# Second layer's attention scores: one head's high and low parts in three products, masks first, turns behind the scores

## What is computed

```
q = concat([rmsnorm(q_nope), rope(rmsnorm(q_pe))])        # 64 + 32 = 96 per head
k = concat([rmsnorm(k_nope), rope(rmsnorm(k_pe))])        # k_pe is one for all heads
s = einsum('bqhd,bkhd->bhqk', qi, k) * scale              # 128 queries at a time
s = where(k_idx <= q_idx, s, -inf)
y = softmax(s) @ v
```

## Time and profile before

| | us |
|---|---|
| median of 3 runs | 2078.09 |
| lowest and highest | 2077.10, 2079.25 |
| the profiled execution, its own time | 2086.7 |
| its span, first to last instruction | 2084.9 |
| TensorE busy in the span | 2047.9 (98%) |
| GpSimd busy | 1515.2 (73%) |
| VectorE busy | 798.8 (38%) |
| ScalarE busy | 503.9 (24%) |

### The profile page before, as it was taken

The page is one execution under the profiler, slowest core; times in us unless marked ns, Lnnn a source line. Parts: engine busy times, 40 slices in busy tenths (PEclk is TensorE's granted clock), DMA queues, the critical chain, the costliest instruction groups (busy, mean ns, idle before and its releaser), DMA issues.

```text
span 2084.9 us, 25564 instructions
## 1 busy us (share of the span) xinstructions
PE 2047.9 (98%) x9848; PEld 1680.3 (81%) x9848; DVE 798.8 (38%) x1254; ACT 503.9 (24%) x981; POOL 1515.2 (73%) x820
## 2 busy tenths in 40 slices
PE   8999999999999999999999999899999999999997
PEld 7888888888888677888888887787788878888887
DVE  4342222211346664222211144865346334555202
ACT  6122111111354543211111133133201142222101
POOL 7787777877877526777878877443588888787775
PEclk9999999999999999999999999999999999999999
DMA  5232323333332102323333332111233322322232
GB/s 171 81 101 91 101 91 101 102 99 90 106 87 91 54 21 72 105 91 101 92 105 100 98 95 90 51 61 47 66 101 91 106 71 102 100 97 95 95 97 82
DMA packets 73884, 187.48 MB, mean 90 GB/s; under 512 B 12096, under 2 KB 27848, under 8 KB 73800
## 3 DMA queue, kind: packets, MB, share of 16 engines
q1 hardware_dynamic: 72632, 183.96, 27.7%
q10 hardware_dynamic: 1168, 2.35, 0.4%
HBM read 184.18 MB, written 2.10 MB: 89 GB/s over the span
## 4 chain that ended last, share of the span: by engine, by line
PE 94%; DVE 3%; ACT 1%; DMA 1%; POOL 1%; issue 1%; SPq 0%; DVEq 0%; ACTq 0%
PE stream_bank L1002 29%; PE stream_bank L1003 29%; PE stream_bank L1004 29%; PE stream_bank L1365 1%; PE work_bank L1695 0%; PE work_bank L1613 0%; DVE s_arena L3007 0%; DMA s_ring<-in_w_even 0%; POOL s_ring_low L829 0%; DVE s_arena L2980 0%; PE work_bank L1403 0%; DVE s_arena L2989 0%; PE work_bank L973 0%; PE work_bank L1714 0%; PE work_bank L1671 0%
## 5 line engine op out<-in xcount | busy, mean ns | idle before, releaser
L827 POOL TENSOR_TENSOR s_ring_high<-s_ring,s_zero 128x1024 fp32r<-128x1024 f32 (+1 forms) x359 | 652.4, 1817 | 487.1 <-DMA s_ring<-in_w_up 132.8
L829 POOL TENSOR_TENSOR s_ring_low<-s_ring,s_ring_high 128x1024 fp32r<-128x1024 f32 (+1 forms) x359 | 825.1, 2298 | 28.1
L1002 PE MATMUL stream_bank<-s_hn,s_ring_high 128*128 128x512 f32 x1682 | 660.8, 393 | 5.0 <-ACT s_arena L2208 2.1
L1004 PE MATMUL stream_bank<-s_hn,s_ring_low 128*128 128x512 f32 x1682 | 655.5, 390 | 0.0
L1003 PE MATMUL stream_bank<-s_hn,s_ring_high 128*128 128x512 f32 x1682 | 655.4, 390 | 0.0
L1002 PEld LDWEIGHTS stream_bank<-s_hn,s_ring_high 128*128 128x128 f32 x1682 | 315.7, 188 | 76.2 <-issue 4.0
L1004 PEld LDWEIGHTS stream_bank<-s_hn,s_ring_low 128*128 128x128 f32 x1682 | 315.7, 188 | 66.7
L1003 PEld LDWEIGHTS stream_bank<-s_hn,s_ring_high 128*128 128x128 f32 x1682 | 315.9, 188 | 65.0 <-issue 0.2
L1002 PE MATMUL stream_bank<-s_act,s_ring_high 128*128 128x512 f32 (+1 forms) x572 | 213.4, 373 | 0.4 <-POOL s_ring_low L829 0.4
L1003 PE MATMUL stream_bank<-s_act,s_ring_high 128*128 128x512 f32 (+1 forms) x572 | 213.2, 373 | 0.0
L1004 PE MATMUL stream_bank<-s_act,s_ring_low 128*128 128x512 f32 (+1 forms) x572 | 213.2, 373 | 0.0
(11 more groups left out here) (454 smaller groups left out, 2356.6 us busy)
## 6 DMA issues: line engine op xcount, KB each, us to landing
s_ring<-in_w_up SPq DMA_DIRECT2D x132, 512.0 KB, 3.5
s_ring<-in_w_down SPq DMA_DIRECT2D x24, 512.0 KB, 3.5
s_ring<-in_w_merge SPq DMA_DIRECT2D x24, 512.0 KB, 3.5
s_ring<-in_w_down SPq DMA_DIRECT2D x24, 448.0 KB, 3.3
s_ring<-in_w_ple SPq DMA_DIRECT2D x20, 512.0 KB, 3.5
s_ring<-in_w_even SPq DMA_DIRECT2D x15, 512.0 KB, 3.5
s_ring<-in_w_odd SPq DMA_DIRECT2D x13, 512.0 KB, 3.6
s_ring<-in_w_down SPq DMA_DIRECT2D x24, 256.0 KB, 2.8
```

The costliest lines, as they stand in the source:

```text
L827: nc.gpsimd.tensor_tensor(hi, ring[:, s, 0:n], zero[:].to_broadcast([P, n]), ALU.add).then_inc(w_high, 1)
L829: nc.gpsimd.tensor_tensor(ring_low[:, s, 0:n], ring[:, s, 0:n], hi.bitcast(F32), ALU.subtract).then_inc(split_ready[s], 1)
L1002: nc.tensor.matmul(o, w(0), x(0), start=start, stop=False)
L1004: return nc.tensor.matmul(o, w(1), x(0), start=False, stop=stop)
```

## The change

Queries and keys of one head at a time are kept in `qk`, four planes of 128 partitions and 512 tokens in the place of `qT` and `kT`: queries high (0) and low (1), keys high (2) and low (3). Partitions 96 to 127 are filled with zeros once, by ACT, behind the table load that opens the stage. ACT rounds the high parts of queries and of keys, each signalled by `qk_high`; DVE makes both low parts and marks the `work` banks done. The scores are three products for each tile, of all 128 rows. The four masks of a head come first, before TensorE waits for its queries and keys; all three `stream` banks are waited for before the first product. TensorE does scores 0 ahead of turn 1, and in the loop turn n + 2 directly behind the scores and what stands beside them, ahead of the gate half and the pair; ACT, DVE and `mla_order` follow. `inter_queries` goes behind the turn.

```diff
     for n in range(MLA_HEADS):
         order += beside_head(n)
+        if n + 2 < MLA_HEADS:
+            order += [("q", n + 2), ("k", n + 2)]
         if n in PAIR_AT:
             order += [("row", PAIR_AT[n]), ("pair", PAIR_AT[n])]
-        if n + 2 < MLA_HEADS:
-            order += [("q", n + 2), ("k", n + 2)]
...
-        qT, at = region(LAT_END - 4 * T, 2, T)
-        kT, at = region(at, 2, T)
+        at = LAT_END - 4 * T
+        qk = nc.alloc_sbuf_tensor_at("s_qk", [P, 4, T], F32R, offset=arena_at + 4 * at)
+        at += 4 * T
@@ TensorE @@
             def head_scores(head):
 
+                for part, (lo, tiles) in enumerate(PROB_PARTS):
+                    g = AG["scores", 3 * head + part]
+                    stream.wait_free(pe, g)
+                    for j, i in enumerate(tiles):
+                        at = PROB_AT[i] - lo + i * P
+                        nc.tensor.matmul(stream.bank(g)[:, at:at + P], ident_b[:], neg_after[:], start=(j == 0), stop=True,
+                                         skip_group_check=True)
                 work.wait_done(pe, AW["q", head])
                 work.wait_done(pe, AW["k", head])
                 for part, (lo, tiles) in enumerate(PROB_PARTS):
                     g = AG["scores", 3 * head + part]
-                    stream.wait_free(pe, g)
                     for i in tiles:
                         at = PROB_AT[i] - lo
-                        nc.tensor.matmul(stream.bank(g)[:, at:at + (i + 1) * P], qT[0:96, head % 2, i * P:(i + 1) * P],
-                                         kT[0:96, head % 2, 0:(i + 1) * P], start=True, stop=True, skip_group_check=True)
-                        mm = nc.tensor.matmul(stream.bank(g)[:, at + i * P:at + (i + 1) * P], ident_b[:], neg_after[:], start=False,
-                                              stop=True, skip_group_check=True)
+                        for q, k in ((0, 2), (0, 3), (1, 2)):
+                            mm = nc.tensor.matmul(stream.bank(g)[:, at:at + (i + 1) * P], qk[:, q, i * P:(i + 1) * P],
+                                                  qk[:, k, 0:(i + 1) * P], start=False, stop=True, skip_group_check=True)
                     mm.then_inc(stream.full[g % BANKS], 1)
@@ TensorE, mla() @@
                 head_turn(0)
                 mo_half(0, 0)
+                head_scores(0)
                 head_turn(1)
-                head_scores(0)
                 mo_half(0, 1)
...
                     if n in (2, 3):
                         for c in range(2 * n - 4, 2 * n - 2):
                             chunk_hidden(c)
+                    if n + 2 < MLA_HEADS:
+                        head_turn(n + 2)
                     for c, half in MO_HALVES.get(n, []):
                         mo_half(c, half)
                     if n in PAIR_AT:
                         pair_out(PAIR_AT[n])
-                    if n + 2 < MLA_HEADS:
-                        head_turn(n + 2)
                     head_turned(n)
@@ ACT @@
             def head_turn(head):
                 m = AW["q", head]
                 work.wait_full(scalar, m)
-                nc.scalar.activation(qT[0:96, head % 2, :], work.bank(m)[0:96, :], ACT.Copy, scale=g_qh).then_inc(
-                    work.done[m % BANKS], 1)
+                nc.scalar.activation(qk[0:96, 0, :], work.bank(m)[0:96, :], ACT.Copy, scale=g_qh).then_inc(qk_high, 1)
+                m = AW["k", head]
+                work.wait_full(scalar, m)
+                if head == 0:
+                    nc.scalar.activation(qk[64:96, 2, :], work.bank(m)[64:96, :], ACT.Copy)
+                nc.scalar.activation(qk[0:64, 2, :], work.bank(m)[0:64, :], ACT.Copy, scale=g_kh).then_inc(qk_high, 1)
@@ ACT, mla() @@
                 scalar.preload_act_table_set("exp_and_others")
+                nc.scalar.activation(qk[96:P], zero[96:P, 0:1].unsqueeze(2).to_broadcast([P - 96, 4, T]), ACT.Copy)
                 head_turn(0)
@@ DVE @@
             def head_turn(head):
 
+                m = AW["q", head]
+                dve.wait_ge(qk_high, 2 * head + 1)
+                nc.vector.scalar_tensor_tensor(qk[0:96, 1, :], work.bank(m)[0:96, :], g_qh, qk[0:96, 0, :].bitcast(F32), ALU.mult,
+                                               ALU.subtract).then_inc(work.done[m % BANKS], 1)
                 m = AW["k", head]
-                work.wait_full(dve, m)
+                dve.wait_ge(qk_high, 2 * head + 2)
                 if head == 0:
-                    for b in range(2):
-                        steps.did(nc.vector.tensor_copy(kT[64:96, b, :], work.bank(m)[64:96, :]))
-                nc.vector.tensor_scalar(kT[0:64, head % 2, :], work.bank(m)[0:64, :], g_kh, None, ALU.mult).then_inc(
-                    work.done[m % BANKS], 1)
+                    steps.did(nc.vector.tensor_tensor(qk[64:96, 3, :], work.bank(m)[64:96, :], qk[64:96, 2, :].bitcast(F32), ALU.subtract))
+                nc.vector.scalar_tensor_tensor(qk[0:64, 3, :], work.bank(m)[0:64, :], g_kh, qk[0:64, 2, :].bitcast(F32), ALU.mult,
+                                               ALU.subtract).then_inc(work.done[m % BANKS], 1)
@@ DVE, mla() @@
                         for h in range(MLSTM_HEADS):
                             take_scores(h)
-                        inter_queries()
...
                             take_hidden(c)
+                    if n + 2 < MLA_HEADS:
+                        head_turn(n + 2)
+                    if n == 0:
+                        inter_queries()
                     for c in mo_ended(n):
                         take_mo(c)
                     if n in PAIR_AT:
                         take_pair(PAIR_AT[n])
-                    if n + 2 < MLA_HEADS:
-                        head_turn(n + 2)
```

More of the change, by code:

```diff
@@ L580, in build @@
         qk_ready = sem("qk_ready")
+        qk_high = sem("qk_high")
         k_scaled = sem("k_scaled")
```

## The result

| | before | changed |
|---|---|---|
| median of six runs each, us | 2078.45 | 2087.51 |
| lowest and highest | 2077.10, 2079.26 | 2086.96, 2088.17 |
| the profiled execution: span | 2084.9 | 2086.3 |
| attention stage, first turn to first product of `odd_out` | 87.65 | 97.89 |

The changed kernel is 9.06 us slower, ratio 1.0038 [1.0026, 1.0050]. The forecast was 2082.8 (2078.09 + 4.7) with a range up to 2086.0: the direction is right, the size is not, and the time is outside the range.

What follows compares the result with a forecast made beforehand. TensorE, 94% of the chain of waits, was taken as the bound. Waits less savings, +1.7 us at the stage's end, and two clock drops, +3.0, made +4.7 on 2078.09: 2082.8 us, range 2077.5 to 2086.0.

Steps and rivals of the forecast that it cites:

- The opening: Before heads 0 and 1: fill, late low parts and DVE's order delay the second head's products; +3.6 us, fill 1.8.
- The wait at 719.39: Before the third head's keys: TensorE's 1.79 us wait goes, as DVE's inter-query products move behind the turn.
- Head 7: Near the end: queries' bank free 0.9 later, gate taken behind low parts; products at about 775.8 against 773.5, +2.3 us.
- the clock: Behind the opening's two new waits, 2.9 and 2.6 us: two drops to half clock at 1.5 us each, +3.0 us.
- head 4's turn: Middle: the turn wants a bank DVE frees behind maxima and a small multiply held up beside GpSimd's split; +0.9 us.
- more collisions: Rival: GpSimd's split meets head 1's small multiply, and a third clock drop follows at head 7; +7.5, 2085.6 us, 15%.
- the three later waits: In a later stage: three waits of 2.3 to 2.5 us, each followed by 3.4 us at 1.2 GHz.
- The saving: Score products of every head: 2.13 us instead of 2.56, saving 0.43 a head, 3.5 in eight.
- The price taken for a 128-column product: Score products: pace taken as 0.09 us, between 0.07 from below and 0.125 from above.
- lower bound of 3.0 us: Score products: the low end of the saving over eight heads, given as 3.0 to 4.0 us.
- The assumption on the profiled execution: Whole kernel: the profiler's addition stays the same, so the span's difference is put on the median; 8.6 us above it before.

Runs made afterwards that it cites:

- e1: Changed kernel with VectorE taking head 0's maxima ahead of head 1's low parts: 2087.21 us, ratio 1.0037 to the kernel before.
- e2: Changed kernel with ScalarE's zero fill of partitions 96 to 127 moved into the projection before: 2085.69 us, ratio 1.0029 to the kernel before.
- e5: Changed kernel with VectorE taking the last chunk's multiply and output bank ahead of head 7's low parts: 2086.65 us.
- e6: Changed kernel with twelve bf16 products, their result overwritten, on TensorE ahead of head 0's masks: 2087.86 us.
- e3: Changed kernel with turns n + 2 back in their old places in the loop on all engines: 2087.40 us.
- e16: Changed kernel with head 4's turn alone back in its old place, behind the pair, on all engines: 2084.80 us.
- e17: Changed kernel with GpSimd's split of one unit of the next stage's weights put off until head 4's high parts are made: 2082.54 us.
- e10: Changed kernel with e1's and e2's edits, turns in old places except head 7's, directly behind head 6's scores: 2077.67 us.
- e9: Changed kernel with e1's and e2's edits, each turn n + 2 directly behind scores n + 1, on ScalarE ahead of that head's exponentials: 2078.03 us.
- e4: Kernel before, fp32 products kept, with only the changed order of turns, scores 0 and inter-query products: 2080.71 us, ratio 1.0006.
- e13: Changed kernel with e1's and e2's edits, head 4's turn in its old place, head 7's directly behind head 6's scores: 2074.07 us.
- e14: Kernel before's fp32 products with masks in front and its opening, turns in the loop placed as in e13: 2074.92 us.

## Why the prediction was wrong in size

**Right.** The opening, step by step: fill 1.92 us (forecast 1.8), head 0's products at 703.97 (703.75), maxima of head 0 behind head 1's low parts, head 1's masks waiting for three banks. The products start at 713.95 (712.2), and 1.5 us of that lateness is the half clock, which the sum counted apart. The wait at 719.39 is gone, and the inter-query products are short. Head 7 waits behind ScalarE and VectorE and for the gate's bank as forecast, 2.9 us against 1.15, with its products at 782.7. In e1, e2 and e5 each repair shortens its own wait or takes it away.

**The step that failed first: the clock.** The forecast took two drops at 1.5 us, +3.0. The profile has four. Each of the two it left out stands behind a wait that the prediction itself had named, head 4's turn and head 7's products; it priced the waits and not what follows them. For head 4's turn the wait was put at 0.9 us, below any that a drop had followed; for head 7 no such reason stands in it. Only the rival "more collisions" had a drop at head 7, with 15% and 2085.6; the drop came, but not that rival's cause, the multiply of head 1 (0.50 us). From TensorE's rows, against the same instructions at full clock: head 0's products 3.50 for 1.99 us, head 1's 3.64 for 2.10, turn 4 and its gate half 5.3 for 3.7, head 7's products 3.51 for 2.09, in sum 6.1 us.

The timed runs agree roughly. The mean granted clock was 0.995 in each of the six of the changed kernel, and 0.9973 as the mean of the 126 of before that stand beside the experiments. The difference of 0.0023 over 2086 us gives an estimate of 4.8 us.

That a drop hangs on TensorE's idle time is shown by e6 for the one at 703.9. The one behind head 4's turn went with its wait in e3, e16 and e17, the one at head 7 with its wait in e10. That a wait of some length is always followed by a drop is not shown: 2.08 us in e2 and 1.79 in before were not, 1.74 in e9 was. The prediction's "2.3 to 2.5 us" for the three later waits are 2.30, 2.18 and 2.11 by the profile's own measure of idle time, so head 7's 2.06 and 0.82 stood close to them.

**The second: head 4's turn.** Forecast +0.9, measured 2.55. The collision was foreseen for the multiply and not for the small sum behind it (L2895), which stands beside the longer half of the split. e16 and e17 give 2.7 and 5.0 us back for it, with the clock behind it. It comes with the order alone, not with the parts: e4 has it.

The Trainium skill, SBUF — State Buffer, section "Who interferes with whom", says that VectorE and GpSimd share one pair of ports as an exclusive lock, and that a VectorE instruction with two inputs in SBUF contends with a GpSimd instruction that reads SBUF. The rows agree: the operations that took 1.10, 2.25 and 2.26 us have both inputs in SBUF, and each ends with an instruction of the split. The low parts, with one input in PSUM, keep their 0.74 us beside the split, as in e9, where it ran from 732.54 to 734.88:

```profile
732.40 0.74 DVE L2818 SCALAR_TENSOR_TENSOR s_qk<-work_bank,s_odd_cols,s_qk 96x512 fp32r<-96x512 f32 x1
733.06 0.73 DVE L2824 SCALAR_TENSOR_TENSOR s_qk<-work_bank,s_odd_cols,s_qk 64x512 fp32r<-64x512 f32 x1
```

Asked of every small operation in the stretch and not of the multiply alone, would have pointed at the second one too: it was held for 2.1 us (2.25 against 0.16).

**The saving: about the right size, another owner.** Forecast 0.43 us a head, from 2.56 to 2.13. From a head's first instruction to the one behind it the changed kernel takes 2.21 in head 6 (before 2.56) and 2.19 in head 3 (before 2.59); up to the second group of hidden products, as above, the saving is 0.47. But 0.21 of that is the masks' place, to which the prediction gave no share. The price taken for a 128-column product, 0.09, was low: in head 2 the starts behind the second and the third of them come after 0.109 and 0.113 us. The prediction's lower bound of 3.0 us for eight heads is also off: with its own upper price of 0.125 the sum gives 8 x (0.43 - 3 x 0.035) = 2.6.

The Trainium skill, TensorE: Matmul & The Clock Gate, section LDWEIGHTS, puts a weight load at its columns over 1.2 GHz, which gives 107 ns for 128. The prediction named it and did not take it; the two paces measured here lie next to it.

**The assumption on the profiled execution.** The prediction took the 8.6 us between the profiled execution of before and its median as what the profiler adds. That is wrong: the changed kernel's lies 0.5 us above its median, and before's was behind the stage 8.7 us longer than that of the changed kernel. It cost nothing here, because the difference was put on the median.

**The sum.** In the stage of the profiled executions: waits 10.7 for 3.8, +6.9; clock +6.1; products and masks 8 x 0.47, -3.8; together 9.2 of the 10.2 us. Of the last 1.0 us, 0.6 lie in masks: head 1's, issued singly as the banks come free, take 0.6 us beside their waits, and head 7's at half clock 0.36, where four in a row take 0.20. The last 0.4 is not placed. In the timed runs it is +9.06. The two steps that failed are 3.1 and 1.65 us; with the forecast's 4.7 they make 9.5.

## What to carry to other kernels

Where an operand gets a second part made by another engine, price the chain that makes it and the banks that it keeps, before the product: here 3.8 us saved cost 6.9 of waits and 5 to 6 of clock. Ask for each wait what the clock does behind it, for all of them and not only the longest, and judge a repair by several executions: the profiled one of e2 is 2.1 us under its median. Then look at what the engine next door does at that moment: putting off one split that nobody needed for 50 us gave 5 us. And run the old arithmetic in the new places: 3.9 of the 4.8 us gained in e13 came with fp32 products too (e14).

## What was not expected of the hardware

- Four bf16 masks of 128 columns cost 0.21 us a head more between fp32 products than in front of them (4.08 against 3.87).
- A multiply of 128x4 took 0.16 us alone and up to 2.31 beside a GpSimd instruction, while the two that held VectorE up in the changed kernel kept their 1.89 and 2.34.
- Waits of nearly one length differed in what followed: 1.74 us in e9 was followed by 3.4 us of half clock, 1.79 in before and 1.78 in e6 were not. At the wait of 3.18 us before head 0's products e17 has 6.8 us of it in one piece, the changed kernel 3.4.
- The granted clock varied between executions of one kernel (0.995 to 0.998 in before's timed runs, with times from 2076.34 to 2085.82), so one profiled span is a poor measure of half a per cent.
